# A hybrid decoder layer on one Trainium2 core: the last gates as seven products of 2x2 blocks, and a scan block every twelve halves

## The reference, cut to what matters

```python
proj = x @ w_in                 # 576 tokens x 2048 -> 10240
u_a, z_a, b_c, c_c, h_c, z_c, g_a, g_c = split(proj)
h[l] = lam * h[l-1] + B @ u_a[l]            # 64 groups of 16 channels, 64 complex states each
y_a = gelu(Re(C @ h) + D * u_a);  y_a = y_a * sigmoid(y_a @ w_glu)
y_a = (y_a * silu(z_a)) @ w_out_a
y_c = (b_c * conv3(c_c * h_c) * silu(z_c)) @ w_out_c
merged = sigmoid(g_a) * y_a + sigmoid(g_c) * y_c
out = layernorm(alpha * x + merged @ w_o)
```

## Time and profile before

| | before |
|---|---|
| median of three runs | 1577.32 us |
| the profiled execution | 1577.16 us, of which span 1575.3 us |
| TensorE busy | 98% of the span, granted clock 0.995 |
| VectorE busy | 830.0 us, 53% |
| ScalarE busy | 444.3 us, 28% |
| GpSimd busy | 189.0 us, 12% |
| DMA | 221 MB, 140 GB/s on the mean |

### The profile page before, as it was taken

One profiled execution on the slowest core, in us unless ns is written; L12 is line 12 of the kernel. 1 busy time (PEld: TensorE's weight loads), 2 busy tenths in 40 slices (PEclk: granted clock), 3 DMA queues, 4 the chain that ended last, 5 costly groups with the idle time before them and its releaser, 6 DMA issues.

```text
span 1575.3 us, 26995 instructions
## 1 busy us (share of the span) xinstructions
PE 1545.9 (98%) x11690; PEld 1539.2 (98%) x11690; DVE 830.0 (53%) x1177; ACT 444.3 (28%) x582; POOL 189.0 (12%) x348
## 2 busy tenths in 40 slices
PE   8999999999999999999999999999999999999994
PEld 8999999999999999999999999999999999999994
DVE  5977374464463553643633533223733355666887
ACT  4222222222122122222222222133411122333444
POOL 0110040230311311302204113010000000000000
PEclk9999999999999999999999999999999999999997
DMA  9352362452543543634625535344544443555573
GB/s 304 125 152 91 92 166 79 116 158 75 133 133 94 146 117 122 176 109 132 161 83 165 136 115 147 104 156 150 189 141 134 125 127 125 160 187 183 183 221 107
DMA packets 87447, 221.21 MB, mean 140 GB/s; under 512 B 19744, under 2 KB 28576, under 8 KB 87328
## 3 DMA queue, kind: packets, MB, share of 16 engines
q1 hardware_dynamic: 71456, 188.78, 38.6%
q0 software_dynamic: 15872, 30.70, 8.6%
HBM read 186.55 MB, written 28.16 MB: 136 GB/s over the span
## 4 chain that ended last, share of the span: by engine, by line
PE 94%; DVE 3%; SPq 1%; DMA 1%; issue 1%; ACT 0%; DVEq 0%
PE acc L634 91%; SPq L420 1%; DMA w_raw<-in_w 1%; PE s_ps L656 1%; DVE r_all L1495 0%; PE s_ps L680 0%; PE s_ps L682 0%; DVE w_lo L979 0%; DVE r_all L1494 0%; PE s_ps L657 0%; PE s_ps L681 0%; PE s_ps L679 0%; PE k_ps L666 0%; DVE rstd L1488 0%; DVE r_all L1460 0%
## 5 line engine op out<-in xcount | busy, mean ns | idle before, releaser
L634 PE MATMUL acc<-xh,w_hi 128*128 128x288 f32 x2560 | 550.9, 297 | 3.9 <-DVE xl L987 3.7
L634 PE MATMUL acc<-xh,w_lo 128*128 128x288 f32 x2560 | 549.5, 296 | 0.0
L634 PE MATMUL acc<-xl,w_hi 128*128 128x288 f32 x2560 | 549.2, 296 | 0.0
L979 DVE TENSOR_TENSOR w_lo<-w_raw,w_hi 128x1024 fp32r<-128x1024 f32 x263 | 321.8, 1224 | 406.8 <-ACT w_hi L764 405.1
L764 ACT ACTIVATE w_hi<-w_raw 128x1024 fp32r<-128x1024 f32 x263 | 278.0, 1058 | 597.3 <-PE acc L634 578.2
L634 PEld LDWEIGHTS acc<-xh,w_hi 128*128 128x128 f32 x2560 | 412.9, 189 | 6.4 <-DVE w_lo L997 2.3
L634 PEld LDWEIGHTS acc<-xh,w_lo 128*128 128x128 f32 x2560 | 413.4, 188 | 0.0
L634 PEld LDWEIGHTS acc<-xl,w_hi 128*128 128x128 f32 x2560 | 413.4, 188 | 0.0
L634 PE MATMUL acc<-mh,w_hi 128*128 128x288 f32 x512 | 152.2, 297 | 1.0 <-DVEq L983 0.7
L634 PE MATMUL acc<-ml,w_hi 128*128 128x288 f32 x512 | 151.3, 296 | 0.0
L634 PE MATMUL acc<-mh,w_lo 128*128 128x288 f32 x512 | 151.3, 296 | 0.0
(11 more groups left out here) (275 smaller groups left out, 1467.1 us busy)
## 6 DMA issues: line engine op xcount, KB each, us to landing
w_raw<-in_w SPq DMA_DIRECT2D x263, 512.0 KB, 3.8
sg_dram<-out_st SPq DMA_DIRECT2D x32, 288.0 KB, 4.6
v_sw<-v_st POOLq DMA_DIRECT2D x32, 144.0 KB, 3.9
gc_in<-sg_dram SPq DMA_DIRECT2D x16, 288.0 KB, 2.7
sz_in<-sg_dram SPq DMA_DIRECT2D x16, 288.0 KB, 2.7
x_in<-in_xT SPq DMA_DIRECT2D x32, 144.0 KB, 2.2
outT<-o_st SPq DMA_DIRECT2D x32, 144.0 KB, 1.8
mb<-mq_dram POOLq DMA_DIRECT2D x8, 512.0 KB, 6.6
```

Of the source, the lines that this page charges most:

```text
L634: ins = pe.matmul(acc[:, par, t, 0:TH], w, m[:, k0 + k, t * TH:(t + 1) * TH], start=first and k == 0 and n == 0, stop=last and k == KH - 1 ...
L979: dve.tensor_tensor(w_lo[h % NW][:, :], w_raw[:, h % NW, :], w_hi[h % NW][:, :].bitcast(F32), ALU.subtract).then_inc(lo_ready, 1)
```

## The change

**Seven products.** The last 28 halves of the gates, which are 14 output blocks, are taken as 7 units n of two output blocks each. The weights of a unit are a 2x2 matrix of tiles A11, A12, A21, A22 (two output blocks by two halves of the inputs), the tokens a 2x2 matrix too (two halves of the inputs by two groups of 288). Instead of eight products of such tiles, a unit forms seven, with sums of weights (S1 to S4, made by DVE in `weight_sums`) and sums of tokens (`x2h`, `x2l`, made once in `token_sums` in halves 122 to 129); the results are put together by seven adds of 128x288 on DVE (c11, c12, c21, c22 are the four quarters of the unit's output). The order of products is A11, A12, S2, S1, S3, S4, A22. Each is 24 matmuls of 128x288 and has its own `w_hi` and `w_lo`, through the same three tiles. A product counts as one half in the numbering, which now runs to 285 in place of 264: the units are halves 132 to 180, and the glu starts at 181 in place of 160. `u_raw` no longer holds the turned states (`st` is `v_sw`).

**The scan.** A block starts every 12 halves in place of 16, and the steps are moved: h = 16 + 12 b + k, with `lch` at 5, `lcl` at 6, `uh` at 6, `states_in` still at 7, the scan at 10, `turn_back` at 13, `hh` at 14, `hl` at 15, `outputs` at 16, the gelu at 18 to 20, the store at 21.

**y.** It is loaded back and split in the last unit (halves 174 to 180) in place of halves 151 to 159.

```diff
+NSG = 7
...
-H_GLU = H_G + 4 * KX
+H_S = H_G + 4 * (KX - NSG)
+H_GLU = H_S + 7 * NSG
...
-SSM_PER = 16
-Y_LOAD = SSM0 + SSM_PER * (BLK - 1) + 23
+SSM_PER = 12
...
+KINDS = ("A11", "A12", "S2", "S1", "S3", "S4", "A22")
+UNIT_AT = {(kind, n): H_S + 7 * n + i for n in range(NSG) for i, kind in enumerate(KINDS)}
+X_SUMS = H_S - 10
+Y_LOAD = UNIT_AT["A11", NSG - 1]
+Y_STEP = (1, 2, 3, 4, 5, 5, 6, 6)
...
         def scan_moves(h):
-            if (b := ssm_step(h, -1)) is not None:
+            if (b := ssm_step(h, 0)) is not None:
                 load_mats(b)
             if (b := ssm_step(h, 2)) is not None:
                 load_u(b)
             if (b := ssm_step(h, 9)) is not None:
                 pool.wait_ge(v_ready, b + 1)
                 swap(v_sw, v_st, v_swapped)
-            if (b := ssm_step(h, 12)) is not None:
+            if (b := ssm_step(h, 21)) is not None:
+                store_y(b)
+            if (b := ssm_step(h, 10)) is not None:
+                store_k(b)
+            if (b := ssm_step(h, 11)) is not None:
                 pool.wait_ge(s_ready, b + 1)
                 swap(v_sw, v_st, s_swapped)
-            if (b := ssm_step(h, 11)) is not None:
-                store_k(b)
-            if (b := ssm_step(h, 13)) is not None:
                 load_lt(b)
-            if (b := ssm_step(h, 25)) is not None:
-                store_y(b)
...
-        for h in range(H_CONV, H_GLU):
+        for h in range(H_CONV, H_S):
             if (b := ssm_step(h, 7)) is not None:
                 states_in(b)
                 taps(b)
-            if (b := ssm_step(h, 19)) is not None:
+            if (b := ssm_step(h, 16)) is not None:
                 outputs(b)
             par = (h // 2) % 2
             if h % 2 == 0:
                 fresh(par)
             half(h, par, xh, xl, h % 2 * KH, h % 2 == 0, h % 2 == 1)
+
+        def product(h, ps, m):
+
+            (mh_, ml_), k0, t = m
+            pe.wait_ge(lo_ready, h + 1)
+            for k in range(KH):
+                wh = w_hi[h % NW][:, k * P:(k + 1) * P]
+                wl = w_lo[h % NW][:, k * P:(k + 1) * P]
+                for i, (w, x) in enumerate(((wh, mh_), (wh, ml_), (wl, mh_))):
+                    ins = pe.matmul(ps, w, of_half(x[:, k0 + k, :], t), start=k == 0 and i == 0,
+                                    stop=k == KH - 1 and i == 2)
+            ins.then_inc(half_done, 1)
+
+        x1, x2 = (xh, xl), (x2h, x2l)
+        for h in range(H_S, H_GLU):
+            kind, n = unit_of(h)
+            if kind == "A11":
+                pe.wait_ge(y_sum, BLK)
+                if n:
+                    pe.wait_ge(s_kept, n)
+                product(h, s_ps[:, 0, 0:TH], (x1, 0, 0))
+            if kind == "A12":
+                if n:
+                    pe.wait_ge(c11_ready, n)
+                product(h, s_ps[:, 1, 0:TH], (x1, KH, 0))
+            if kind == "S2":
+                pe.wait_ge(xs_low, KH)
+                if n:
+                    pe.wait_ge(e_ready, n)
+                product(h, s_ps[:, 2, 0:TH], (x2, 0, 0))
+            if kind == "S1":
+                fresh(1)
+                product(h, acc[:, 1, 0, 0:TH], (x2, 0, 1))
+            if kind == "S3":
+                product(h, acc[:, 1, 1, 0:TH], (x2, KH, 1))
+            if kind == "S4":
+                fresh(0)
+                product(h, acc[:, 0, 0, 0:TH], (x1, KH, 1))
+            if kind == "A22":
+                product(h, acc[:, 0, 1, 0:TH], (x2, KH, 0))
...
         def scan_steps(h):
-            if (b := ssm_step(h, 19)) is not None:
+            if (b := ssm_step(h, 16)) is not None:
                 act.wait_ge(y_done, b + 1)
...
-            if (b := ssm_step(h, 4)) is not None:
+            if (b := ssm_step(h, 5)) is not None:
                 act.wait_ge(lc_ready, b + 1)
                 if b:
...
                 act.wait_ge(lb_ready, b + 1)
                 act.activation(lbh[:, :, :], mb[:, :, :, :].rearrange("p g c s -> p g (c s)"), ACT.Copy)\
                    .then_inc(lbh_ready, 1)
+            if (b := ssm_step(h, 6)) is not None:
                 act.wait_ge(u_loaded, U_LOAD * (b + 1))
                 act.activation(uh, u_raw[:, :, :], ACT.Copy).then_inc(uh_ready, 1)
...
-            if (b := ssm_step(h, 15)) is not None:
+            if (b := ssm_step(h, 14)) is not None:
                 act.wait_ge(st_ready, b + 1)
                 act.activation(last_state[:, b * NG:(b + 1) * NG, :], st[:, :, CP - 1:], ACT.Copy)
...
+        def weight_sums(h):
+
+            for kind, of, to in (("S3", "A11", "A21"), ("S2", "S3", "A22"), ("S1", "A21", "A22"), ("S4", "S2", "A12")):
+                n, r_ = divmod(h - H_S - SUM_STEP[kind], 7)
+                if r_ or not 0 <= n < NSG:
+                    continue
+                dve.wait_ge(lo_ready, h + 3)
+                if kind in ("S3", "S2"):
+                    dve.wait_ge(group_loaded[to, n % 2], 16 * (n // 2 + 1))
+                dve.tensor_tensor(raw_of(kind, n), raw_of(of, n), raw_of(to, n), ALU.add).then_inc(weight_sum, 1)
+                dve.wait_ge(weight_sum, sum_count(kind, n))
...
-            if (b := ssm_step(h, 17)) is not None:
+            if (b := ssm_step(h, 15)) is not None:
                 dve.wait_ge(hh_ready, b + 1)
                 own.mark(dve.tensor_tensor(hl[:, :, 1:CP], st[:, :, 0:CP - 1], hh[:, :, 1:CP].bitcast(F32), ALU.subtract))
...
-            if (b := ssm_step(h, 5)) is not None:
+            if (b := ssm_step(h, 6)) is not None:
                 dve.wait_ge(lch_ready, b + 1)
                 dve.tensor_tensor(lcl[:, :, :, :].rearrange("p g t c -> p g (t c)"),
...
+            kind, n = unit_of(h)
+            m = first + 2 * n
+            ps = {"A12": s_ps[:, 1, 0:TH], "S2": s_ps[:, 2, 0:TH], "S1": acc[:, 1, 0, 0:TH], "S3": acc[:, 1, 1, 0:TH],
+                  "S4": acc[:, 0, 0, 0:TH], "A22": acc[:, 0, 1, 0:TH]}.get(kind)
+            k_s, k_e, k_f = (t[:, :] for t in keep)
+            o1, o2 = out_st[m % 4], out_st[(m + 1) % 4]
+            if kind != "A11":
+                dve.wait_ge(half_done, h + 1)
+            if kind == "A12":
+                dve.wait_ge(s_kept, n + 1)
+                out_free(m)
+                dve.tensor_tensor(of_half(o1, 0), k_s, ps, ALU.add).then_inc(c11_ready, 1)
+            if kind == "S2":
+                dve.tensor_tensor(k_e, k_s, ps, ALU.add).then_inc(e_ready, 1)
+            if kind == "S1":
+                dve.wait_ge(e_ready, n + 1)
+                dve.tensor_tensor(k_f, k_e, ps, ALU.add).then_inc(f_ready, 1)
+            if kind == "S3":
+                dve.wait_ge(f_ready, n + 1)
+                out_free(m + 1)
+                dve.tensor_tensor(of_half(o2, 1), ps, k_f, ALU.subtract).then_inc(c22_ready, 1)
+                dve.wait_ge(c11_ready, n + 1)
+                dve.tensor_tensor(k_s, ps, k_e, ALU.subtract).then_inc(g_ready, 1)
+                dve.wait_ge(c22_ready, n + 1)
+                dve.wait_ge(g_ready, n + 1)
+                free(1)
+            if kind == "S4":
+                dve.tensor_tensor(of_half(o1, 1), k_f, ps, ALU.add).then_inc(c12_ready, 1)
+            if kind == "A22":
+                dve.tensor_tensor(of_half(o2, 0), k_s, ps, ALU.add).then_inc(c21_ready, 1)
+                dve.wait_ge(c12_ready, n + 1)
+                dve.wait_ge(c21_ready, n + 1)
+                free(0)
+            for i, step in enumerate(Y_STEP):
+                if h == Y_LOAD + step:
+                    dve.wait_ge(yh_ready, i + 1)
+                    dve.tensor_tensor(yl[:, i, :], y_in[i % 2][:, :], yh[:, i, :].bitcast(F32), ALU.subtract)\
+                       .then_inc(yl_ready, 1)
...
+        def load_y(n):
+            if n < 2:
+                sp.wait_ge(y_stored, U_LOAD * BLK)
+                sp.wait_ge(lo_ready, UNIT_AT["S3", NSG - 2] + 1)
+            else:
+                sp.wait_ge(yl_ready, n - 1)
+            sp.dma_start(y_in[n % 2][:, :], y_dram[n]).then_inc(y_loaded[n % 2], 16)
```

More of the change, by code:

```diff
@@ L79, in ssm_step, with unit_of, sum_count, raw_count @@
     return b if r == 0 and 0 <= b < BLK else None
+def unit_of(h):
+    return KINDS[(h - H_S) % 7], (h - H_S) // 7
+SUM_STEP = {"S3": -2, "S2": -1, "S1": 0, "S4": 1}
+def sum_count(kind, n):
+    return sum(1 for k, at in SUM_STEP.items() for v in range(NSG)
+               if 7 * v + at < 7 * n + SUM_STEP[kind]) + 1
+def raw_count(h):
+    return sum(1 for g in range(h % NW, h + 1, NW) if not H_S <= g < H_GLU)
 class Steps:
@@ L376, in build @@
     norm_ready = sem("norm_ready")
+    xs_loaded = [sem(f"xs_loaded{i}") for i in range(2)]
+    xs_sums = sem("xs_sums")
+    xs_high = sem("xs_high")
+    xs_low = sem("xs_low")
+    group_loaded = {(kind, p): sem(f"group_{kind}_{p}") for kind in ("A11", "A12", "A21", "A22") for p in range(2)}
+    weight_sum = sem("weight_sum")
+    s_kept = sem("s_kept")
+    e_ready = sem("e_ready")
+    f_ready = sem("f_ready")
+    g_ready = sem("g_ready")
+    c11_ready = sem("c11_ready")
```

(38 more changed lines are left out.)

192 lines of the change are left out of this document (138 added, 54 removed).

## The result

| | before | after |
|---|---|---|
| median | 1577.36 us (4 runs, 1576.9 to 1578.0) | 1619.84 us (4 runs, 1617.59 to 1622.03) |
| the profiled execution | 1577.16 us, span 1575.3 | 1617.59 us, span 1615.8 |
| granted clock over the span | 0.995 | 0.974 |
| ratio | | 1.0269, 95% interval 1.0251 to 1.0287 |

What follows compares the result with a forecast made beforehand. TensorE, busy for 98% of the span, was taken as the bound. -22.4 + 18.5 + 5.5 + 1.0 + 2.3 = +4.9 us on 1577.3 gave 1582.2 us, range 1573 to 1591, the forecast's own 1578 to 1587.

Steps and rivals of the forecast that it cites:

- Part 1: Gates' seven units: 168 fewer matmuls at 0.1333 us each, a gain of 22.4 us.
- Part 2: Scan outputs: TensorE waits for `hl` behind a half's end at six blocks, a loss of 18.5 us.
- Part 3: Scan states: TensorE waits for late `lbl` and `ul` at five blocks, 8.9 us replacing 3.4, net loss 5.5 us.
- For b = 0, 2, 4 (place 5) ... nothing: Scan states of these blocks: ScalarE waits for nothing, operands end near +5.9 where +6.1 is due, no loss.
- Part 4: Gates' units: VectorE and ScalarE hand operands to each other, loss 1.0 us; bounds 0 and 1 us per unit in six.
- The rival that it bounds the products: Gates' units: engines' hand-over limits the products above 0.4 us of extra latency; 1587 to 1592 us, chance 0.14.
- Part 5: Glu's first half: `y`, loaded in the last unit, comes 1.6 to 2.9 us late; loss taken as 2.3 us.
- by less than its weights' slack: Glu's first loads: they end later too, but relative to the delayed TensorE by less than that slack; no loss added.
- The clock falls in the new gaps: Scan: TensorE's clock falls to its lower level behind the new gaps, 10 us more, 1592 us; chance 0.05.
- each of the four longest gaps is followed by 5 us of it: Scan: 5 us at the lower clock behind each of the four longest gaps, 4 x 2.5 = 10 us.
- At the lower level matmuls take double: TensorE in the scan: at the lower clock level (1.2 GHz) a matmul takes double its time.
- a clock of a scan window under 1.00: Scan in the new profile: a granted clock under 1.00 in a window would make the prediction fall.

Runs made afterwards that it cites:

- experiment 3: Changed kernel with `hl` on VectorE and `lch`, `lbh` on ScalarE issued ahead of the half's result: 1562.76 us, ratio 0.990.
- experiment 6: Kernel before with the new scan step table, `hl`, `lch` and `lbh` ahead of the half's result, still eight products: 1578.93 us, ratio 1.0004.
- experiment 5: Changed kernel with idle matmuls in TensorE's row ahead of the scan's states only, not its outputs: 1614.02 us, ratio 1.0229.
- experiment 7: Kernel of experiment 3 with SyncE asking for the first glu operands without waiting for the gates' last stores: 1560.04 us, ratio 0.988.
- experiment 8: Kernel of experiment 7 with `w_o` begun in the other `acc` bank and `lcl` made behind `ul`: 1554.52 us, ratio 0.985.
- experiment 4: Changed kernel with idle matmuls in TensorE's row ahead of the scan's states and outputs: 1587.32 us, ratio 1.0057.
- experiment 2: Changed kernel with VectorE's `hl` issued ahead of the half's result: 1580.6 us, ratio 1.001.

## Why the prediction was right in sign and wrong in size

**Part 1, the products (-22.4): right.** 168 fewer matmuls, and the 1176 of the units start within 156.9 us (963.4 to 1120.3), 0.133 us each. Experiments 3 and 6 differ by it, less its known side effects.

**Part 2, the outputs (+18.5): right**, +17.9. 3.40, 2.50 and 2.73 lost against 3.51, 2.59 and 2.84; same places, same chain. (No row here shows its 0.06 us "for one more wait", nor the 0.05 of part 4; both are too small to matter.)

**Part 3, the states (+5.5): right for the five gaps named** (net +5.7), and its step "For b = 0, 2, 4 (place 5) ... nothing" failed for block 0, +1.8. VectorE's and ScalarE's rows there, of the changed kernel:

```profile
152.03 0.29 DVE L1410 TENSOR_TENSOR bbar<-scr,scr 128x128 f32<-128x128 f32 x1
...
152.36 1.06 ACT L954 ACTIVATE lch<-lc 128x1024 fp32r<-128x1024 f32 x1 [5.88 <-DVE bbar L1410]
153.32 1.04 ACT L958 ACTIVATE lbh<-mb 128x1024 fp32r<-128x1024 f32 x1
...
154.27 1.04 ACT L927 ACTIVATE w_hi<-w_raw 128x1024 fp32r<-128x1024 f32 x1
155.22 0.67 ACT L962 ACTIVATE u<-u_raw 128x576 fp32r<-128x576 f32 x1
155.35 1.23 DVE L1175 TENSOR_TENSOR w_lo<-w_raw,w_hi 128x1024 fp32r<-128x1024 f32 x1 [1.22 <-ACT w_hi L927]
156.49 1.22 DVE L1466 TENSOR_TENSOR lcl<-lc,lch 128x1024 fp32r<-128x1024 f32 x1
157.62 1.22 DVE L1472 TENSOR_TENSOR lbl<-mb,lbh 128x1024 fp32r<-128x1024 f32 x1
158.76 0.75 DVE L1475 TENSOR_TENSOR u<-u_raw,u 128x576 fp32r<-128x576 f32 x1
```

The sum took the place 5 of a running scan, where `lch` waits for nothing. In block 0 it waits for VectorE's matrices, and the whole row starts later: `ul` ends at 159.5 where TensorE was due at 157.84.

**Part 4, the hand-over (+1.0): 0**, the lower bound. The rival that it bounds the products is out.

**Part 5, y (+2.3): the right stage, mostly the wrong wait.** y was in time, by a hair: its loads took 2.7 to 3.1 us (median 2.9) where the earlier trace rows gave 4.1, and "0 with a quick DMA" came true. The step that failed is its last sentence, that the first loads of the glu end later "by less than its weights' slack". It looked at the loads' own lateness and not at what SyncE waits for ahead of them, the stores of the last unit's two gates, over 6 us of DMA. The two gaps of the stage cost 4.5 us in this profile. The first goes with the stores: in experiment 5's profile, where the code here is the same, SyncE's loads followed the stores 7.0 us behind instead of 8.1, and the gap was 0.71 us instead of 1.95. Not all of the 4.5 us is that wait, though: with the loads asked for earlier, gaps of 2.13 us (experiment 7) and of 1.09 and 1.58 us (experiment 8) were left. Another 1.1 us came at `w_o`, which no part had: nobody counted the parity of the halves.

**The clock: the step that decided.** The forecast took the granted clock as 1.00 in the scan and so put the term at nothing; this is the step that failed, and it measured 31.9 us. The rival "The clock falls in the new gaps" had a chance of 0.05 and a price of 10 us. Its mechanism is the one that experiment 4 shows, and it was priced too low by a factor of three: "each of the four longest gaps is followed by 5 us of it" was ten gaps followed by 6.8 us on average, 31 to 32 us. ("At the lower level matmuls take double" is nearly so: 0.24 us for 0.133.) The last line of the prediction names the right sign, a clock of a scan window under 1.00. Without the clock the same sum would read 1577.4 + 8.6 = 1586.0, inside the range, though partly by luck: block 0, the glu stage and `w_o` cost 5.1 us more than foreseen, and parts 2 and 4 cost 1.6 less.

The Trainium skill's page "TensorE: Matmul & The Clock Gate", Part 1, which the prediction cited, advises against idle gaps in TensorE's work about as long as the longest ones here. The trace agrees as far as that goes: behind each of the nine gaps of 3.5 us in these profiles the clock fell. But it also fell behind 25 of the 39 gaps of 1.7 to 2.9 us, which that advice leaves out, and seven of the ten falls in the changed kernel's profile are of this kind; here the measurement decides. The prediction had the row that warned of it and the longest gap it would create, and still gave the rule one chance in twenty. Behind its first 20 us the kernel before had no gap above 1.33 us in TensorE's work to test it on, and that absence was evidence of nothing.

## What to carry to other kernels

A wait on a saturated TensorE can be priced twice: once by its length, and (here from a gap of 1.7 us on) once by the granted clock behind it. Look at the mean clock of each stage before and after; when "busy" grows while instructions fall, it is the clock. In a row of an in-order engine, put what another engine waits for *ahead* of the taking of a result that itself waits for that engine: two such moves turned +2.7% into -1.0%. And when work is moved, read the queue that carries the loads behind it for what it waits on, not only for how long it takes.

## What the runs showed of the hardware

The clock's fall is neither certain nor proportional to the gap. These are the gaps of 0.8 us and more in TensorE's work (from start to start, between 20 and 1500 us) in the nine profiled executions of the changed kernel and the experiments, and behind how many of them the granted clock fell to 0.50, 2.3 to 5.3 us after the gap's start:

| gap, us | gaps | followed by a fall |
|---|---|---|
| 3.5 | 9 | 9 |
| 2.4 to 2.9 | 14 | 10 |
| 2.0 to 2.3 | 13 | 10 |
| 1.7 to 1.95 | 12 | 5 |
| 0.8 to 1.6 | over 20 | 0 |

Two equal gaps of one execution can differ in this (block 1's states and block 3's in experiment 2, both 2.0 us: low clock behind the first, none behind the second). The kernel with several gaps near 2 us had the wider spread of times (ten runs over 14 us in experiment 2, four runs within 1.2 us with the gaps filled in experiment 4), so a single profile of it says little. That idle matmuls on data already there hold the clock up, and leave the waits as long as they were, was shown by experiments 4 and 5. It gives back 32.5 of the 57 us that taking the waits away gives (experiment 3).

What stays open: what makes the clock fall behind one gap of 1.7 to 2.9 us and not behind its twin, and why the stretch from 224.1 to 234.4 us is longer than that from 405.0 to 411.8, both behind gaps of 3.53 us. Gaps of chosen lengths in an otherwise unbroken kernel were not tried.
